# The weight ring of a two-layer encoder kernel: four slots instead of five

## The chip, the cores and the metric

The kernel runs on one core of one Trainium2 chip. The metric is the device time of one execution in microseconds (us). Three runs of the kernel before took 1249.94, 1251.59 and 1251.48 us (median 1251.48). All times below are read from one profiled execution of it.

## The reference

Two layers of a hybrid encoder on 256 tokens of 1024 channels, all in float32. Cut to what matters:

```python
for l in range(2):
    x = LN(alpha * x + 0.5 * swiglu(x, w_gate[l, 0], w_up[l, 0], w_down[l, 0]))      # D_FF = 2816
    p = x @ w_in[l]               # 2824 columns: diff-attention q, k, v; mLSTM q, k, v, gates; S5 input
    x = LN(alpha * x + concat(diff_attention(p), mlstm(p), s5(p)) @ w_out[l])
    q, kv = x @ xattn_wq[l], mem @ xattn_wkv[l]                                       # 256 memory rows
    x = LN(alpha * x + softmax(q k / 16) v @ xattn_wo[l])
    x = LN(alpha * x + 0.5 * swiglu(x, w_gate[l, 1], w_up[l, 1], w_down[l, 1]))
```

The weights, about 200 MB, are read from HBM once; activations stay in SBUF.

## The kernel before

**Units.** Each product with a weight matrix is cut into units. A unit is a piece of weights of 128 partitions by 2048 float32 columns, 1 MB (ten units are half as large). There are 198 units in one fixed order, written out by hand (`unit_order`). In the text F0 is the first FFN of a layer and F1 the second; each has 33 units, three for every block of 256 hidden channels: gate and up for the first half of the input channels, gate and up for the second half, and down. Between the FFNs stand the units of the mix (`w_in` pieces DV, DQ, DK, SU, MQ, MK, MM, then `w_out` pieces W), of the cross attention (WQ, WO), and sixteen K and V units of the memory, which need no activations and are put where TensorE (PE) would have to wait for a chain on other engines (`FILL`).

**The way of a unit.** Four engines work on it. SyncE (SP) loads it with two DMAs into a ring slot `RAW[u % RING]` (`load`, line 402). ScalarE (ACT) copies the slot to `WH[u % RING]`, rounding to the fp32r type that PE multiplies in (`split`, line 1226). VectorE (DVE) writes the rest, RAW minus WH, back over RAW as `WL` (`split`, line 1654). PE then multiplies three times per chunk (high by high, high by low, low by high: lines 518 to 520) and adds one to `unit_used` with the last matmul of the unit. The slot is free then, and not before: `load(u)` waits until `unit_used` is at least `u - RING + 1`, which with a ring of five is the end of unit u-5.

**The order on the engines.** No engine chooses its order at run time. ACT and DVE have one list each, in which the splits stand between all their other work: the SiLU and product of the FFN (`silu`, `h_mul`), the transposing of the FFN's hidden block (`turn_h` on PE in F0, sixteen DVE transposes in F1) and its own split into HH (ACT, `h_hi`) and HL (DVE, line 1650), which PE needs before the down unit; layer norms (`boundary`); RoPE (`swap_copy`, a matmul at line 908, `rope`), the S5 recurrence (`s5_states`), softmaxes (`diff_exp`, `diff_mix`), and in F0 the preparing of the S5 tables on DVE (`prepare_...`, `tables`, after blocks 0 to 6, `skip_taps` before the last). An ACT list entry "split" waits for the landing of its unit, and what stands behind it in the list waits too.

In one FFN block j the ACT list is: HH of block j, split, two SiLUs of block j+1, split, split. The DVE list is: HL of block j, split, two products of block j+1, split, (F1: the sixteen transposes of block j+1), split, (F0: a piece of table work). PE's own list is: gate/up unit, gate/up unit, wait for HH and HL, down unit.

**POOL.** GpSimd loads parameters and layer norm vectors. At the start its DMAs wait for chosen ring slots to be filled a given number of times, so that they go behind the first weights; the units meant are 2, 5, 7 and 9.

Of the kernel before, what the change touches and what calls it, by code (L numbers as in the profile page):

```python
# [44 lines left out]
LAMBDA_INIT = [0.8 - 0.6 * math.exp(-0.3 * l) for l in range(DEPTH)]  # L45


RING = 5
FFN_UNITS = 3 * BLOCKS
FILL = {("mix", 0): [(0, "K", 0), (0, "K", 1)],  # L50
# [60 lines left out]
def build(nc, x_in, mem_in, wg, wu, wd, ln_g, ln_b, w_in, w_out, wq, wkv, wo, par, const, out):  # L111
# [12 lines left out]
    with ctx:  # L124
        top = [(nc.sbuf_base + 31) // 32 * 32]

        def place(name, shape, dt, at=None):
            size = 4 * int(np.prod(shape[1:]))
            if at is None:
                at = top[0]  # L130
                top[0] += (size + 31) // 32 * 32
            return nc.alloc_sbuf_tensor_at(name, shape, dt, offset=at), at

        def sb(name, shape, dt=F32, at=None):
            return place(name, shape, dt, at)[0]
# [6 lines left out]
        ML = sb("ML", [P, KC, SEQ], F32R)  # L142
        slots = [place(f"RAW{s}", [P, 2048], F32) for s in range(RING)]
        RAW = [slot for slot, _ in slots]
        WL = [sb(f"WL{s}", [P, 2048], F32R, at) for s, (_, at) in enumerate(slots)]
        WH = [sb(f"WH{s}", [P, 2048], F32R) for s in range(RING)]
        LNGB, gb_at = place("LNGB", [P, 2, D], F32)
# [104 lines left out]

        raw_loaded = [Event(f"raw_loaded{s}", 0) for s in range(RING)]
        split_hi = Event("split_hi", 0)
# [143 lines left out]
        def _(sp):  # L398
# [3 lines left out]
            def load(u, first, second):  # L402

                if u >= RING:
                    sp.wait_ge(unit_used.sem, u - RING + 1)
                for dst, src in (first, second):
                    sp.dma_start(dst, src).then_inc(raw_loaded[u % RING].sem, 16)  # L407

# [1939 lines left out]
        def _(pool):  # L2348
# [86 lines left out]
            def load_params(l):  # L2435

                pool.dma_start(PAR[:, :], par[l, :, 0:P_END]).then_inc(param_in.sem, 16)
                pool.dma_start(PDL[:, :], par[l, :, P_DL:P_DL + 256]).then_inc(param_in.sem, 16)
                if l == 0:
                    pool.wait_ge(raw_loaded[0].sem, 64)  # L2440
                pool.dma_start(PB[96:128, :, :, :].rearrange("c (a i) t n -> c a (i t n)", a=4),
                               par[l, :, P_B:P_B + 512].rearrange("(a c) n -> c a n", a=4)).then_inc(rest_in.sem, 16)
                pool.dma_start(PCB[:, :], par[l, :, P_C:P_C + 1024]).then_inc(rest_in.sem, 16)
                pool.dma_start(iota[:, :], const[:, K_IOTA:K_IOTA + STEPS]).then_inc(rest_in.sem, 16)

            pool.wait_ge(raw_loaded[2].sem, 32)
            load_params(0)
            pool.wait_ge(raw_loaded[2].sem, 64)
            pool.dma_start(kst[:, P:K_END], const[:, P:K_END]).then_inc(const_rest.sem, 16)
            pool.wait_ge(raw_loaded[4].sem, 64)  # L2450
            for l in range(DEPTH):
                count["n"] = 0
                layer["l"] = l
# [22 lines left out]
                if l + 1 < DEPTH:  # L2476
                    load_params(l + 1)
# [72 lines left out]
```

## Time and profile before

| | |
|---|---|
| time, median of three runs | 1251.48 us |
| the profiled execution: its own time | 1249.85 us |
| its span | 1248.0 us |
| PE busy | 1226.9 us (98%) |
| DVE busy | 874.5 us (70%) |
| ACT busy | 600.0 us (48%) |
| POOL busy | 156.1 us (13%) |
| read from HBM | 217.34 MB, 175 GB/s over the span |
| chain that ended last | PE 96%, all else 4% |

The span is what the profile covers, the time holds 1.85 us more around it. Busy time counts instructions of an engine; the granted TensorE clock was 0.999 over the span. The chain that ended last is followed back from the last instruction, at each step to what released it.

### The profile page before, as it was taken

How to read it: one execution, taken by the hardware profiler on the slowest of the kernel's cores; microseconds unless marked ns; L12 is line 12 of the kernel's file. 1: busy time of each engine (PE TensorE's matmuls, PEld its weight loads, DVE VectorE, ACT ScalarE, POOL GpSimd, SP SyncE). 2: the span in 40 equal slices, each digit the busy share in tenths (PEclk: the TensorE clock that was granted, in tenths of full speed). 3: DMA queues.
4: the chain of work that ended last, by engine and by line, in shares of the span. 5: the costliest groups of instructions: out<-in, count | busy, mean ns of one | idle time of the engine just before them, and what ended most of it. 6: DMA issues, size and time to landing. Idle time of an engine off the chain costs nothing.

```text
span 1248.0 us, 16328 instructions
## 1 busy us (share of the span) xinstructions
PE 1226.9 (98%) x6616; PEld 1052.0 (84%) x6616; DVE 874.5 (70%) x1337; ACT 600.0 (48%) x731; POOL 156.1 (13%) x161
## 2 busy tenths in 40 slices
PE   7999999999999999999999999999999999999997
PEld 6888888998889888888888888889987998788886
DVE  5677747687565668888856676665776756988885
ACT  5444554557444554443445344545556445544442
POOL 1026800000102000000000067300001100000000
PEclk9999999999999999999999999999999999999999
DMA  9755555542456366566666555645323635655560
GB/s 336 266 169 188 183 169 169 169 131 72 138 200 216 102 228 210 186 187 200 202 203 193 179 197 174 192 151 185 113 102 120 196 124 158 212 187 186 200 203 34
DMA packets 160234, 219.45 MB, mean 176 GB/s; under 512 B 6912, under 2 KB 136064, under 8 KB 160160
## 3 DMA queue, kind: packets, MB, share of 16 engines
q1 hardware_dynamic: 156864, 206.60, 51.0%
q0 software_dynamic: 3152, 11.76, 2.9%
q8 instruction: 52, 0.85, 0.3%
q14 instruction: 22, 0.18, 0.0%
q10 hardware_dynamic: 144, 0.07, 0.0%
HBM read 217.34 MB, written 1.05 MB: 175 GB/s over the span
## 4 chain that ended last, share of the span: by engine, by line
PE 96%; SPq 1%; DMA 1%; issue 1%; ACT 1%; DVE 1%; DVEq 0%; POOLq 0%; POOL 0%
PE PS L518 28%; PE PS L520 28%; PE PS L519 28%; PE PS L1141 1%; PE PS L1165 1%; PE PS L601 1%; PE PS L931 1%; PE PS L549 1%; DMA RAW<-in_ffn_w_down 1%; SPq L407 1%; PE PS L831 1%; PE PS L843 1%; PE PS L864 1%; PE PS L908 1%; PE PS L781 0%
## 5 line engine op out<-in xcount | busy, mean ns | idle before, releaser
L1650 DVE TENSOR_TENSOR WL<-RAW,WH 128x2048 fp32r<-128x2048 f32 (+1 forms) x199 | 447.4, 2254 | 170.4 <-ACT WH L1222 169.3
L1222 ACT ACTIVATE WH<-RAW 128x2048 fp32r<-128x2048 f32 (+1 forms) x199 | 370.8, 1872 | 164.4 <-DMA RAW<-in_ffn_w_up 129.3
L518 PE MATMUL PS<-WH,XH 128*128 128x512 f32 x762 | 302.3, 397 | 1.7 <-DVE WL L1650 1.4
L520 PE MATMUL PS<-WH,XL 128*128 128x512 f32 x762 | 297.3, 390 | 0.0
L519 PE MATMUL PS<-WL,XH 128*128 128x512 f32 x762 | 297.2, 390 | 0.0
L518 PEld LDWEIGHTS PS<-WH,XH 128*128 128x128 f32 x762 | 143.4, 188 | 32.5 <-DVE WL L1650 1.8
L520 PEld LDWEIGHTS PS<-WH,XL 128*128 128x128 f32 x762 | 143.2, 188 | 30.3
L519 PEld LDWEIGHTS PS<-WL,XH 128*128 128x128 f32 x762 | 143.5, 188 | 28.8 <-issue 0.5
L518 PE MATMUL PS<-WH,HH 128*128 128x512 f32 x352 | 137.8, 392 | 1.2 <-issue 1.1
L520 PE MATMUL PS<-WH,HL 128*128 128x512 f32 x352 | 137.1, 389 | 0.0
L519 PE MATMUL PS<-WL,HH 128*128 128x512 f32 x352 | 137.0, 389 | 0.0
L1810 DVE STREAM_TRANSPOSE PS<-HB 32x128 f32<-32x128 f32 x320 | 103.3, 323 | 4.7
L518 PE MATMUL PS<-XH,WH 128*128 128x256 f32 x320 | 94.1, 294 | 0.0
L2420 POOL TENSOR_TENSOR SM<-SM,half_c 128x1 f32<-128x1 f32 x16 | 12.9, 804 | 643.8 <-DVE SM L1705 643.8
L519 PE MATMUL PS<-XL,WH 128*128 128x256 f32 x320 | 90.5, 283 | 0.0
L520 PE MATMUL PS<-XH,WL 128*128 128x256 f32 x320 | 90.5, 283 | 0.0
L1316 ACT ACTIVATE SG<-PS 128x256 f32<-128x256 f32 x88 | 33.7, 383 | 114.8 <-PE PS L520 114.8
L1222 ACT ACTIVATE HH<-PS 128x512 fp32r<-128x512 f32 x44 | 26.3, 599 | 112.5 <-PE PS L549 57.7
L518 PEld LDWEIGHTS PS<-WH,HH 128*128 128x128 f32 x352 | 66.1, 188 | 16.1 <-issue 2.7
L520 PEld LDWEIGHTS PS<-WH,HL 128*128 128x128 f32 x352 | 66.1, 188 | 13.9
L519 PEld LDWEIGHTS PS<-WL,HH 128*128 128x128 f32 x352 | 66.1, 188 | 13.5
L519 PEld LDWEIGHTS PS<-XL,WH 128*128 128x128 f32 x320 | 61.3, 192 | 1.6 <-issue 1.4
(352 smaller groups left out, 1790.6 us busy)
## 6 DMA issues: line engine op xcount, KB each, us to landing
RAW<-in_ffn_w_down SPq DMA_DIRECT2D x88, 512.0 KB, 4.4
RAW<-in_ffn_w_gate SPq DMA_DIRECT2D x87, 512.0 KB, 4.0
RAW<-in_ffn_w_up SPq DMA_DIRECT2D x87, 512.0 KB, 5.0
RAW<-in_w_in SPq DMA_DIRECT2D x44, 512.0 KB, 4.5
RAW<-in_xattn_wkv SPq DMA_DIRECT2D x32, 512.0 KB, 4.2
RAW<-in_xattn_wq SPq DMA_DIRECT2D x16, 512.0 KB, 4.3
RAW<-in_w_out SPq DMA_DIRECT2D x12, 512.0 KB, 4.5
RAW<-in_xattn_wo SPq DMA_DIRECT2D x12, 512.0 KB, 4.0
```

The lines of the kernel that those rows point to most:

```text
L407: sp.dma_start(dst, src).then_inc(raw_loaded[u % RING].sem, 16)
L518: nc.tensor.matmul(out_ap, sh, mh, start=first, stop=False)
L519: nc.tensor.matmul(out_ap, sh, ml, start=False, stop=False)
L520: return nc.tensor.matmul(out_ap, sl, mh, start=False, stop=last)
L549: mm = nc.tensor.transpose(PS[:, 6, fc * SEQ + t * P:fc * SEQ + t * P + P], HB[:, t, fc * P:fc * P + P], ident)
L601: mm = nc.tensor.transpose(PS[:, 4 + 2 * t + half, i * P:i * P + P], X[:, t, c * P:c * P + P], ident)
L831: mm = nc.tensor.matmul(PS[0:32, 7, j * P:j * P + P], PCB[:, o:o + 32], CQ[:, part, i, 0:TAPS, :].rearrange("p a c -> p (a c)"), start=(pa ...
L1222: return nc.scalar.activation(dst, src, ACT.Copy)
L1316: nc.scalar.activation(SG[:, t, :], PS[:, 4 + t, 0:FB], ACT.Silu).then_inc(sg_done.sem, 1)
L1650: return v.tensor_tensor(dst, full, hi.bitcast(F32), ALU.subtract)
L1810: ins = v.transpose(dst[:, :, :, 32 * i:32 * i + 32], src[:, :, :, 32 * j:32 * j + 32])
L2420: g.tensor_tensor(SM[:, 22 + t:23 + t], SM[:, 20 + t:21 + t], half_c[:, 0:1], ALU.pow).then_inc(ln_root.sem, 1)
```

## The change

The ring gets four slots for RAW/WL and four for WH. Everything that is placed behind them in SBUF moves down by one slot of each. `load(u)` waits for the end of unit u-4. The order of units and every engine's list stay as they are. POOL's three waits name another slot and count: slot 1 filled twice is unit 5 (before slot 0 twice), slot 3 twice is unit 7 (before slot 2 twice), slot 1 three times is unit 9 (before slot 4 twice).

```diff
-RING = 5
+RING = 4
...
                 if l == 0:
-                    pool.wait_ge(raw_loaded[0].sem, 64)
+                    pool.wait_ge(raw_loaded[1].sem, 64)
...
             load_params(0)
-            pool.wait_ge(raw_loaded[2].sem, 64)
+            pool.wait_ge(raw_loaded[3].sem, 64)
             pool.dma_start(kst[:, P:K_END], const[:, P:K_END]).then_inc(const_rest.sem, 16)
-            pool.wait_ge(raw_loaded[4].sem, 64)
+            pool.wait_ge(raw_loaded[1].sem, 96)
```

## Rows read from the trace of the kernel before

**Rows 1.** Page, busy us (share of the span) and instructions of each engine.

```profile
PE 1226.9 (98%) x6616; PEld 1052.0 (84%) x6616; DVE 874.5 (70%) x1337; ACT 600.0 (48%) x731; POOL 156.1 (13%) x161
```

**Rows 2.** Waits of SP's queue: waited for: us in total, times, longest us.

```profile
SPq L407 <- PE PS L520: 1000.5, 190, 21.6
```

**Rows 3.** Page, costliest groups: busy, mean ns of one | idle before, releaser.

```profile
L1650 DVE TENSOR_TENSOR WL<-RAW,WH 128x2048 fp32r<-128x2048 f32 (+1 forms) x199 | 447.4, 2254 | 170.4 <-ACT WH L1222 169.3
L1222 ACT ACTIVATE WH<-RAW 128x2048 fp32r<-128x2048 f32 (+1 forms) x199 | 370.8, 1872 | 164.4 <-DMA RAW<-in_ffn_w_up 129.3
```

**Rows 4.** Page, DMA issues: count, KB each, median us to landing.

```profile
RAW<-in_ffn_w_down SPq DMA_DIRECT2D x88, 512.0 KB, 4.4
...
RAW<-in_ffn_w_up SPq DMA_DIRECT2D x87, 512.0 KB, 5.0
```

**Rows 5.** Timeline of SP's queue, F1 of layer 0: start us, us, issue.

```profile
510.86 0.38 SPq L407 DMA_DIRECT2D RAW<-in_ffn_w_gate  x1
...
527.18 0.38 SPq L407 DMA_DIRECT2D RAW<-in_ffn_w_gate  x1
```

**Rows 6.** Timeline of DVE, the same block: start us, us, operation.

```profile
515.41 5.37 DVE L1810 STREAM_TRANSPOSE PS<-HB 32x128 f32<-32x128 f32 x16
```

**Rows 7.** Timelines of SP's queue and DVE, a block of F0, layer 1.

```profile
727.88 0.37 SPq L407 DMA_DIRECT2D RAW<-in_ffn_w_gate  x1
...
739.24 0.38 SPq L407 DMA_DIRECT2D RAW<-in_ffn_w_gate  x1
...
729.64 2.47 DVE L1650 TENSOR_TENSOR WL<-RAW,WH 128x2048 fp32r<-128x2048 f32 x1 [2.68 <-ACT WH L1222]
...
735.99 0.69 DVE L1650 TENSOR_TENSOR HL<-PS,HH 128x512 fp32r<-128x512 f32 x1
```

**Rows 8.** Timelines of SP's queue and DVE, start of F1, layer 0.

```profile
464.03 0.38 SPq L407 DMA_DIRECT2D RAW<-in_ffn_w_gate  x1
...
469.05 0.42 DVE L1799 TENSOR_TENSOR HB<-SG,PS 128x256 f32<-128x256 f32 x1
```

**Rows 9.** Timelines of SP's queue, ACT and PE, around the SU unit, layer 0.

```profile
242.02 0.92 SPq L407 DMA_DIRECT2D RAW<-in_w_in  x2
...
242.41 0.58 ACT L1222 ACTIVATE XE<-PS 128x512 f32<-128x512 f32 x1
...
244.70 1.02 PE L908 MATMUL PS<-XE,kst 128*128 128x512 f32 x2
```

**Rows 10.** Timelines of SP's queue, DVE and PE, from MQ on, layer 0.

```profile
260.73 0.88 SPq L407 DMA_DIRECT2D RAW<-in_w_in  x2
...
254.67 4.49 DVE L1650 TENSOR_TENSOR WL<-RAW,WH 128x2048 fp32r<-128x2048 f32 x2 [3.06 <-ACT WH L1222]
...
271.53 0.75 DVE L2051 SCALAR_TENSOR_TENSOR PR<-PR,SM 128x128 f32<-128x128 f32 x2
...
276.72 0.49 PE L942 MATMUL PS<-kst,PR 128*128 128x128 f32 x3
```

**Rows 11.** Timelines of SP's queue, ACT and PE, end of cross attention, layer 1.

```profile
1050.90 0.37 SPq L407 DMA_DIRECT2D RAW<-in_ffn_w_gate  x1
...
1045.40 1.92 ACT L1222 ACTIVATE WH<-RAW 128x2048 fp32r<-128x2048 f32 x1 [2.55 <-DMA RAW<-in_ffn_w_up]
...
1053.44 1.03 PE L601 MATMUL PS<-kst,X 128*128 128x128 f32 x8
```

**Rows 12.** Timeline of PE at the start.

```profile
11.69 0.59 PE L518 MATMUL PS<-WH,XH 128*128 128x512 f32 x1
12.12 0.39 PE L519 MATMUL PS<-WL,XH 128*128 128x512 f32 x1
12.35 0.40 PE L520 MATMUL PS<-WH,XL 128*128 128x512 f32 x1
```

**Rows 13.** Stretches: us, busy (instructions) PE PEld DVE ACT POOL, PEclk, DMA.

```profile
1240.40:1244.30 3.90, 0.00 (x0) 0.00 (x0) 3.17 (x7) 1.24 (x2) 0.55 (x1) 1.00 0.33 134
1244.30:1248.00 3.70, 0.00 (x0) 0.00 (x0) 1.27 (x2) 0.00 (x0) 0.00 (x0) 0.50 0.38 142
```

## The prediction

> **What bounds the kernel now.** I read the page's engine rows first: PE is busy 98% of the span and all others have room [rows 1]. The kernel can therefore be slower only by making PE wait. Then the waits of SP's queue: 190 loads stood, 1000.5 us in all, until PE had let go of a slot [rows 2]. So every load is issued at the end of a unit, and the ring's size sets of which one. The costliest groups come third: one split costs ACT 1.87 us and DVE 2.25 us, and ACT's idle time ahead of its splits is mostly a wait for a landing, 129.3 us [rows 3]. ACT is thus not late by its own work in the FFNs; it stands at a split until the unit is there, with its list behind it. In the timelines last I looked, at each split, for when its slot was let go and what stands behind it.
>
> **What the change moves.** 194 loads are issued one unit later. From the release to the landing a gate/up unit takes 0.42 us (its second DMA is issued that much later) and 5.0 us, 5.4 in all; a down unit 0.4 and 4.4, so 4.8 to 4.9 [rows 4]; for the `w_in`, K and V units I read 4.9 to 5.3 and for half units 3.4. A full unit of PE's work is 5.44 us, a third of the block of 16.32 between the two issues of [rows 5]. Where ACT now waits for a landing its split starts 5.4 us later. Weights themselves stay early enough: DVE finished its split 9 to 13 us before PE took the unit in the steady blocks, and 5.4 off that leaves 4 or more. What counts is what stands behind the splits in two lists that can't be reordered. I went through both lists with the release of unit u-4 in place of u-5, all durations kept, and noted where PE comes first. POOL's waits still mean the same units; its next result that PE needs had over 20 us to spare, cost 0. The lower SBUF addresses: no row connects time with an address, 0; bounds -1 and +1 us (the spread of the three runs). The terms:
>
> A. *Start of an FFN* (4 times). The first split in the FFN's list is the unit b+4 (b its first unit); behind it stand the second SiLU, the second product and, in F1, the transposes. Unit b+4 can now be issued only when unit b ends. Layer 0, F1: issue 464.03, landed 469.4, ACT to 471.4, DVE to 473.7, product at 474.1, where it ended at 469.47 before and PE used it at once [rows 8]: 4.7 us. The same sum gives 4.7 for F0 of layer 1, 3.7 for F1 of layer 1 (it already waited there 1.4 us) and 3.9 at the very start, where the queue is empty when unit 4 goes out. Together 17.0.
>
> B. *Blocks of F0 with table work on DVE.* The chain: release, landing 5.45, ACT 1.92, DVE 2.29, table work W, HL 0.68, and 0.1 for the handovers, 10.45 + W. PE has, from the release to the down unit, 739.24 - 727.88 = 11.36 us. The table work is the DVE time between the third split's end and HL: 735.99 - (729.64 + 2.47) = 3.9 in the block shown [rows 7], with which the chain is 14.1 (the landing there 5.2): PE waits 2.7. For the seven such blocks of layer 1 the waits are 3.3, 2.7, 3.4, 2.7, 2.1, 1.4, 2.4 (W from 4.3 down to 2.5; the later blocks give PE 11.8), in layer 0 3.4, 2.8, 3.6, 2.5, 2.1, 1.3, 2.4, and 0.5 in each eighth block by ACT's own table work. Each wait stands alone: the next chain starts from PE's end of the down unit. Together 37.1. The blocks without table work, and the chain to the two products (10.5 against 10.9), cost nothing while a landing takes under 5.8.
>
> C. *Last block of an FFN.* PE goes there from one down unit to the next, so the last split, 5.0 + 1.9 + 2.3 after a release, then `skip_taps` (2.1 us, F0 only) and HL end 4.2 us after PE in three of four FFNs (4.0 in layer 1's F0; the last FFN has no unit left to split): 12.3.
>
> D. *Steady blocks of F1.* DVE's chain: release, down unit landed 4.9, ACT 1.9, DVE 2.3, transposes 5.37 [rows 6], split 2.2, HL 0.68, handovers 0.2: 17.55 against PE's 16.32 [rows 5]. The chain starts at a release ahead of the wait, so a block that waited 1.2 gives the next 1.2 more: every second block pays. Nine blocks, 6.0 us for each F1, 12.0.
>
> E. *Mix.* Here the loads that ACT's list wants early are the costly ones. The split of DQ's second half stands in front of the copy XE for the swap matmul in SU: released at 242.02, it lands at 247.2, ACT is done at 249.1 and XE at 249.7, while PE comes at 244.7 [rows 9]: 4.95. The split of MM's first unit stands in front of `s5_states` on DVE: before, DVE had it in the pair at 254.67, ahead of MQ's end at 260.73; now it waits for that end, so (with PE 4.95 late) it lands at 270.8 and DVE is done at 275.1 instead of 259.1. `s5_states`, `diff_max` and `diff_mix` take the 13.2 us to 272.3 before, 288.3 now; PE wants the result at 276.7, now 282.1 [rows 10]: 6.2, and 0.45 on the way. That is 11.6 in each layer. Layer 1 has no memory units in the middle of its mix, its splits of W come long after their landing, and it pays no more. Layer 0 has four such units, and the same pattern goes on, each time a split that waits for the unit PE has just ended, with the work that PE wants next behind it: K2 and K3 before the third swap copy 0 and the fourth 4.9; V0 before the second `diff_exp` 5.0; W1 before the third 3.75; W2 before the copy AT of head 2, 6.95, and the decay scores 1.0; W3 before AT of head 3, 5.7. Together 39.1 for layer 0, 50.7 for both.
>
> F. *Around the cross attention.* WQ0's split stands before the layer norm's square: 1.4 and 1.2. The last WO unit comes 1.85 late, twice. At its end two splits stand before the square of the next norm. In layer 1 the second was done at 1045.40; now it waits for the release of 1050.90 (+1.85), so the split ends at 1060.1, square, root and scale at 1063.6, and PE, which went on at 1053.44 [rows 11], waits 8.3. Layer 0 by the same sum 5.7, where K units lie between. Together 20.3.
>
> G. *The clock.* The waits above hold 11 of 4.7 us or more. At the end of the trace PE does nothing from 1240.4 on; the granted clock is 1.00 for 3.9 us and 0.50 after that [rows 13]. So a long wait can leave PE at 1.2 GHz. Priced by the start: until 12.1 us a matmul starts every 0.43 us, after it every 0.23 [rows 12]; that went on for 4.4 us of products there, a loss of 4.4 x (1 - 0.23/0.43) = 2.0 us. Eleven times is 22; the bounds are 0 and 31 (7 us at the lower clock each). I take half, 11: not each wait need lower it, and while PE is slow the other lists catch up.
>
> The Trainium skill, "TensorE: Matmul & The Clock Gate", section "Why this matters for your kernels", says that an idle gap between bursts of matmuls puts the array back to its lower clock. By that rule G would be near its 22; the trace agrees only with its last idle stretch.
>
> Sum: A 17.0, B 37.1, C 12.3, D 12.0, E 50.7, F 20.3: 149.4; G 11: 160. On the profiled execution's 1249.85 that is 1410; the median of the runs is 1.6 us above it, so I say 1411.
>
> **Rivals.**
> 1. *The clock holds.* G is 0: 1400. For it: inside the span the granted clock never moved, with waits up to 1.4 us. Against: [rows 13].
> 2. *The clock drops at nearly each long wait and nothing is got back*: 149 + 22 to 31, so 1422 to 1431.
> 3. *The FFN lists take it up.* The waits of B, C and D are differences of a few us between two chains of 10 to 17. If landings with one slot less in flight took 3.5 instead of 5.4, D would vanish and B and C shrink by 1.9 each: 17 blocks times 1.9 less, A 8 less: about 1250 + 160 - 12 - 32 - 8, 1358. For it: the fourth and fifth load share the engines at times. Against: at one unit per 5.4 us and 5.0 to landing hardly two overlap now.
> 4. *Not slower.* Four slots are read as enough, because a unit's DVE split stays 4 us or more ahead of PE, and PE is the only bound: 1250. At the start it could even gain, with one load less ahead of the parameter loads, up to the 1.4 us that PE waits for a split there. It decides if no entry behind a waiting split is the next thing that PE needs; [rows 8] and [rows 9] show a margin of 0.1 and 1.7 us, against 5. The Trainium skill, "Trainium Kernel Development and Optimization", section "Best Practices", advises double buffering for the overlap of DMA with compute. By it four slots are plenty and the time is this rival's; the trace speaks against it with the 129 us that ACT stands at landings with five.
> 5. *More cascades than I found*: late entries met by landings of 6 us and more (they occur, up to 10.8 where POOL loads at the same time), 10 to 20% on 149: 1425 to 1450.
>
> **How the numbers follow.** Forecast 1411: 0.42. Clock holds 0.20. Clock in full 0.12. Shorter landings 0.11. More cascades 0.12. Not slower 0.02, the last 0.01 for something in between. The range 1368 to 1440 takes in rivals 1 and 2, both bounds of G, and errors of a fifth downward in the sum of A to F; outside are rival 4, the lower part of 3 and the upper part of 5. Within 0.2%, 2.5 us, is what this kernel's measurement can't tell from no change: slower 0.97, same 0.02, faster 0.01.
>
> **What would show it.** PE's busy share falls to about 88 to 90%. ACT's waits for landings grow from some 165 us to well over 300. New waits of PE: for DVE's HL in F0's blocks 1 to 7 (2 to 3.5 us each), none in F0's block 9, every second block in F1; the swap matmul at line 908 about 5 us; the transposes at line 942 in the mix; line 601 before F1 of layer 1 about 8. Layer 0's mix grows three times as much as layer 1's. The PE clock shows stretches below 1.0 behind the long waits. Wrong would be: weights themselves (DVE WL) as the main releaser of PE; the FFN blocks unchanged; landings shorter than 4.5 us.

## The result, and the profile after

| | before | four slots |
|---|---|---|
| time, median | 1250.79 us | 1462.11 us (1457.5 to 1466.46, 4 runs) |
| ratio | | 1.169, 95% interval 1.1675 to 1.1704 |
| span of the profiled execution | 1248.0 us | 1461.7 us |
| mean granted clock | 0.999 | 0.947 |

The change costs 211 us. 160 us were forecast, with a range up to 1440, and the time lies 22 us above it.

The engine rows of the profile page after, to set beside [rows 1]:

```profile
PE 1299.2 (89%) x6616; PEld 1093.9 (75%) x6616; DVE 870.2 (60%) x1337; ACT 596.0 (41%) x731; POOL 144.1 (10%) x161
```

This row splits the loss. PE does the same 6616 matmuls and is busy 72.3 us longer (1226.9 before). Its idle time is 1461.7 - 1299.2 = 162.5 us, where it was 21.1: 141.4 us more. The two make 213.7, the whole difference of the spans. Waits were forecast at 149.4 and the clock at 11, so the waits hold and the clock does not.

What PE waited for, after (us in total, times, longest us); of these only line 601 on the constants, the first wait of the kernel, was there before at this size:

```profile
PE PS L518 <- issue: 62.3, 33, 4.1
PE PS L942 <- DVE PR L2051: 20.7, 4, 5.9
PE PS L908 <- ACT XE L1222: 15.1, 4, 4.9
PE PS L518 <- DVE HB L1799: 14.3, 5, 4.2
PE PS L950 <- ACT AT L1222: 12.3, 2, 7.1
PE PS L601 <- DVE X L1711: 10.8, 2, 8.0
PE PS L518 <- DVE WL L1650: 7.6, 5, 2.2
PE PS L601 <- DMA kst<-in_constants: 4.9, 1, 4.9
```

The weights themselves (DVE WL) are 7.6 us of it. The rest are results that stand behind a split in a list: the FFN's HH and HL ahead of a down unit (most of the 33 times "issue", by which the profile means that it shows no releaser; in the block below PE starts 0.1 us behind HL), the mixed softmax PR, the swap copy XE, the product HB at an FFN's start, the copy AT, the norm's X.

Waits of SP's queue, the costliest groups and the landings, after, to set beside [rows 2 to 4]:

```profile
SPq L407 <- PE PS L520: 1222.0, 191, 22.3
```

```profile
L1650 DVE TENSOR_TENSOR WL<-RAW,WH 128x2048 fp32r<-128x2048 f32 (+1 forms) x199 | 446.5, 2247 | 437.1 <-ACT WH L1222 436.2
L1222 ACT ACTIVATE WH<-RAW 128x2048 fp32r<-128x2048 f32 (+1 forms) x199 | 371.8, 1872 | 616.2 <-DMA RAW<-in_ffn_w_up 305.1
```

```profile
RAW<-in_ffn_w_down SPq DMA_DIRECT2D x88, 512.0 KB, 4.3
...
RAW<-in_ffn_w_up SPq DMA_DIRECT2D x87, 512.0 KB, 5.0
```

ACT stands idle 616.2 us ahead of its splits, 164.4 before. A landing takes what it took: 5.0 and 4.3 us against 5.0 and 4.4.

One block of F0 in layer 1, the timelines of SP's queue, ACT, DVE and PE after (start us, us, operation, idle before and its releaser), which answers to [rows 7]:

```profile
834.36 0.38 SPq L407 DMA_DIRECT2D RAW<-in_ffn_w_gate  x1
834.78 0.51 SPq L407 DMA_DIRECT2D RAW<-in_ffn_w_up  x1
...
841.16 1.92 ACT L1222 ACTIVATE WH<-RAW 128x2048 fp32r<-128x2048 f32 x1 [11.30 <-DMA RAW<-in_ffn_w_up]
...
843.11 2.29 DVE L1650 TENSOR_TENSOR WL<-RAW,WH 128x2048 fp32r<-128x2048 f32 x1 [10.93 <-ACT WH L1222]
...
848.91 0.69 DVE L1650 TENSOR_TENSOR HL<-PS,HH 128x512 fp32r<-128x512 f32 x1
...
849.69 0.77 PE L518 MATMUL PS<-WH,HH 128*128 128x512 f32 x1 [3.99 <-issue]
```

Released and issued at 834.4, landed at 841.1 (one of the long landings, 6.8 us), ACT to 843.1, DVE to 845.4, 3.5 us of table work, HL to 849.6; PE was there at 845.7. The swap matmul in SU answers to [rows 9]:

```profile
285.98 0.92 SPq L407 DMA_DIRECT2D RAW<-in_w_in  x2
...
291.25 1.91 ACT L1222 ACTIVATE WH<-RAW 128x2048 fp32r<-128x2048 f32 x1 [5.62 <-DMA RAW<-in_w_in]
293.07 0.58 ACT L1222 ACTIVATE XE<-PS 128x512 f32<-128x512 f32 x1
...
293.70 2.08 PE L908 MATMUL PS<-XE,kst 128*128 128x512 f32 x2 [4.87 <-ACT XE L1222]
```

4.87 us were measured, 4.95 forecast. The row holds the second loss too: the two matmuls take 2.08 us, and took 1.02 before. The stretches around it (us, busy and instructions of PE PEld DVE ACT POOL, PEclk, DMA share, GB/s):

```profile
288.83:293.70 4.87, 0.00 (x1) 0.00 (x1) 1.53 (x3) 2.39 (x2) 0.00 (x0) 0.85 0.35 123
293.70:299.00 5.30, 5.30 (x19) 4.27 (x20) 4.36 (x5) 0.00 (x0) 0.00 (x0) 0.50 0.02 3
299.00:303.00 4.00, 4.00 (x36) 3.37 (x36) 1.63 (x8) 2.75 (x7) 0.00 (x0) 1.00 0.41 115
```

While PE waited the clock fell to 1.2 GHz (0.50). The counts of these rows can't be set against each other, since the shapes differ; the pace of one shape, 128x256, can. It starts every 0.21 us at 1.2 GHz and every 0.12 us at 2.4:

```profile
297.07 0.41 PE L519 MATMUL PS<-XL,WH 128*128 128x256 f32 x1
297.28 0.41 PE L520 MATMUL PS<-XH,WL 128*128 128x256 f32 x1
...
299.37 0.28 PE L519 MATMUL PS<-XL,WH 128*128 128x256 f32 x1
299.49 0.28 PE L520 MATMUL PS<-XH,WL 128*128 128x256 f32 x1
```

The trace has 26 such stretches, 150 us together, besides the one behind the last matmul. Half of 150 is 75, and PE's added busy time is 72.3.

By stages, cut at the ends of units in both traces (us; idle and busy are PE's):

| stage | before | after | more idle | more busy |
|---|---|---|---|---|
| F0, layer 0 | 205.5 | 248.5 | 27.3 | 15.7 |
| mix and cross attention, layer 0 | 249.5 | 317.0 | 43.6 | 23.9 |
| F1, layer 0 | 181.5 | 198.3 | 12.1 | 4.6 |
| F0, layer 1 | 191.3 | 235.8 | 29.1 | 15.3 |
| mix and cross attention, layer 1 | 217.1 | 248.0 | 22.0 | 8.9 |
| F1, layer 1 | 183.2 | 194.1 | 7.1 | 3.8 |

### The profile page after: what moved, and what is told of

Its sections match the earlier page's. It is cut to its first block, busy times and chain, and to the rows that moved or that the text cites. A ratio compares the mean times of both kernels' runs of the same rounds, so it can differ in the third digit from the quotient of the medians.

```text
span 1461.7 us, 16328 instructions
## 1 busy us (share of the span) xinstructions
PE 1299.2 (89%) x6616; PEld 1093.9 (75%) x6616; DVE 870.2 (60%) x1337; ACT 596.0 (41%) x731; POOL 144.1 (10%) x161
## 4 chain that ended last, share of the span: by engine, by line
PE 74%; DMA 9%; issue 6%; DVE 5%; ACT 5%; SPq 1%; POOL 0%; DVEq 0%; POOLq 0%; ACTq 0%
PE PS L518 22%; PE PS L520 21%; PE PS L519 21%; ACT WH L1222 2%; DMA RAW<-in_ffn_w_up 2%; DMA RAW<-in_xattn_wkv 2%; DMA RAW<-in_w_in 2%; DVE WL L1650 2%; DMA RAW<-in_ffn_w_down 1%; PE PS L1141 1%; DMA RAW<-in_w_out 1%; PE PS L908 1%; PE PS L1165 1%; SPq L407 1%; PE PS L601 1%
## 5 line engine op out<-in xcount | busy, mean ns | idle before, releaser
L1222 ACT ACTIVATE WH<-RAW 128x2048 fp32r<-128x2048 f32 (+1 forms) x199 | 371.8, 1872 | 616.2 <-DMA RAW<-in_ffn_w_up 305.1
L518 PE MATMUL PS<-WH,XH 128*128 128x512 f32 x762 | 306.8, 403 | 15.6 <-DVE HB L1799 14.3
L518 PE MATMUL PS<-WH,HH 128*128 128x512 f32 x352 | 150.7, 428 | 62.4 <-issue 61.0
L518 PEld LDWEIGHTS PS<-WH,XH 128*128 128x128 f32 x762 | 145.4, 191 | 48.3 <-DVE HB L1799 15.3
L519 PE MATMUL PS<-WL,HH 128*128 128x512 f32 x352 | 145.4, 413 | 0.0
L520 PE MATMUL PS<-WH,HL 128*128 128x512 f32 x352 | 145.3, 413 | 0.0
L518 PEld LDWEIGHTS PS<-WH,HH 128*128 128x128 f32 x352 | 71.4, 203 | 92.0 <-issue 76.3
L518 PE MATMUL PS<-XH,WH 128*128 128x256 f32 x320 | 98.2, 307 | 0.5 <-DVE ZT L1941 0.5
L520 PEld LDWEIGHTS PS<-WH,HL 128*128 128x128 f32 x352 | 71.1, 202 | 16.5
L519 PEld LDWEIGHTS PS<-WL,HH 128*128 128x128 f32 x352 | 71.9, 204 | 14.3
L518 PEld LDWEIGHTS PS<-XH,WH 128*128 128x128 f32 x320 | 64.7, 202 | 3.2 <-issue 2.0
L520 PEld LDWEIGHTS PS<-XH,WL 128*128 128x128 f32 x320 | 64.3, 201 | 0.0
```

Source lines behind the costliest of these rows:

```text
L518: nc.tensor.matmul(out_ap, sh, mh, start=first, stop=False)
L519: nc.tensor.matmul(out_ap, sh, ml, start=False, stop=False)
L520: return nc.tensor.matmul(out_ap, sl, mh, start=False, stop=last)
L1222: return nc.scalar.activation(dst, src, ACT.Copy)
```

## The experiments

Each kernel was timed beside the kernel before, whose medians there are 1249.8 to 1250.1 us.

**1. The issue alone.** Five slots at their old places, but each load waits for the unit it would wait for with four:

```diff
-                if u >= RING:
+                if u >= RING - 1:
+                    sp.wait_ge(unit_used.sem, u - RING + 2)
+                elif u >= RING:
                     sp.wait_ge(unit_used.sem, u - RING + 1)
```

> Five slots at the old addresses, but each load from unit 4 on waits for the unit that it would wait for with four slots. POOL's own waits are those of the kernel before. Theory (the later issue alone makes the loss, by the entries behind the waiting splits and by the clock): 1462 us, within 5. Rival (the overlap of slots or the moved SBUF addresses have a part): clearly below 1462; if they had all of it, 1251.

Measured 1461.61 us (1457.24 to 1463.72), ratio 1.168 [1.166, 1.171]. The whole loss is the later issue; slots, addresses and POOL's waits have no part that shows.

**2. The FFNs' loads alone.** As 1, with `ORDER[u][1] in ("F0", "F1")` added to the condition.

> Five slots; only the loads of FFN units (F0 and F1) wait as with four. In the changed kernel PE's waits grew by 75.6 us inside the four FFNs and its busy time, by the clock, by 39.4 us. The last wait of each F0 hangs on a unit of the mix and should stay away (two times 3.7 to 4.0 us and some 3 us of clock). Theory (the parts are separate and add): 1251 + 115 - 14 = 1352 us, between 1340 and 1362, and the mix keeps its old length. Rival (parts feed each other, a late load shifts all that follow on the queue): over 1370.

Measured 1366.08 us, ratio 1.092 [1.090, 1.094], 4 us above the stated range. Layer 0's mix and cross attention kept their 249.5 us exactly. The excess is at two places that I had not counted: the first units of an FFN are loaded in the stage ahead of it, so the norm before F0 of layer 1 was late (PE waited 3.88 us, and 2.8 us more busy time) and the one before F1 of layer 1 as well (7.94 us, and 2.1). Added to 1352 these give 1369. The parts add, but a load's wait falls where its split stands.

**3. Four loads of 198.** As 1, for unit b+4 of each FFN only (term A).

> Five slots; only four loads of 198, the unit b+4 at the start of each FFN (term A), wait as with four. Theory: PE waits 3 to 4.7 us at each of the four places and the clock takes some 2 to 3.5 us behind three or four of them: 14 to 17 + 6 to 12, so 1271 to 1280 us. Rival 1 (the price of a wait is the wait itself): 1265 to 1268. Rival 2 (later loads of the ring absorb it): 1251 to 1256.

Measured 1274.57 us (1273.89 to 1274.74), ratio 1.019 [1.018, 1.021]. PE's idle time grew by 14.9 us and its busy time by 9.1. Rivals 1 and 2 of this run are out: the late loads cost their waits and three fifths more. One of the five falls of the clock in this trace (1.6 of the 9.1 us) is not at a late load. It stands behind a wait of 1.36 us in the mix of layer 1, which the kernel before has too, with no fall behind it.

**4. Matmuls in the waits.** Four slots; matmuls without use (one operand zero, or a result that is overwritten) ahead of most awaited products, each group sized to the wait of the changed kernel, for example ahead of the down unit in F0's blocks 1 to 7:

```diff
+            def keep_busy(n, b, src, first):
+                for _ in range(n):
+                    nc.tensor.matmul(bank(b), ZERO[:, :], src[:, 0:2, :].rearrange("p c n -> p (c n)"),
+                                     start=first, stop=first)
...
                     gate_up(b + 3 + 3 * j, 1)
+                    if s == 0 and j <= 7:
+                        keep_busy((13, 10, 14, 9, 7, 4, 9)[j - 1], 0, XH, False)
                     h_turned(l, s, j)
```

> Four slots as in the changed kernel; PE gets matmuls of 128x512 with no use (zeros added to its own accumulators, or results that the next product overwrites) ahead of most waits: at each FFN start 7 to 15, ahead of the down unit in F0's blocks 1 to 7 4 to 14, in each last block 7 or 14, ahead of swap copies 0 and 2 17 or 18, ahead of two attention products 28 and 20. Each group is sized to end just before the awaited result. Lines 942 and 601 get none. Theory (the added busy time of 72 us is the lower clock, and the clock falls because PE pauses): the waits stay as long, about two thirds of the 152 us at the lower clock vanish, 45 to 55 us: 1407 to 1417 us. Rival (the clock falls for another reason, such as the load of the whole chip, or filler delays the real work): 1455 or more.

Measured 1447.41 us, a miss by 30 us. The trace tells why. In the F0s, where every larger wait was filled, no stretch at 1.2 GHz is left (12 in the changed kernel), and the stages took 236.0 and 223.4 us instead of 248.5 and 235.8. But the groups at the swap copies stood at copies 0 and 2, where PE does not wait at all. They added 12.2 us, and the waits at copies 1 and 3 stayed with their stretches. So the mechanism held and my placing was wrong, which the next kernel puts right (groups at copies 1 and 3):

> The filler kernel with two groups moved, which had stood at swap copies 0 and 2 where PE doesn't wait (12.2 us of added work, 53 matmuls of 0.23 us) and now stand at copies 1 and 3, in their waits of 4.7 us. Theory (each wait over some 2 us lowers the clock, and matmuls in the wait keep it up): 12.2 us of work less and the three stretches of 7 us at the lower clock behind these waits gone (10 us), so 1425 us, 1419 to 1431. Rival (the clock in the mix falls whatever PE does there): 1435.

Measured 1431.5 us (1428.62 to 1433.12): 15.9 less than the run before it, where 22 were expected, and half a us above the range at its median. The stretches behind these three waits are gone. Of ten left, one is behind the last matmul, eight follow waits without matmuls in them (lines 942 and 601 above all), and one a last block of F0 where 2.5 us of the wait stayed unfilled.

**5. The same in the small kernel.** Kernel 3 with 15, 15, 15 and 7 matmuls in its four waits.

> The kernel with four late loads (1274.6 us), and 15, 15, 15 and 7 matmuls of 128x512 in front of the awaited product at the four places, whose results the next product overwrites; 0.23 us each, within the waits of 4.1, 4.3, 4.0 and 2.1 us. Theory (the waits cost themselves plus a stretch at the lower clock that comes from PE's pause): the waits stay, the stretches go, 1274.6 - 8 = 1266 to 1268. Rival (the stretch comes whatever PE does there): 1274 to 1276.

Measured 1268.07 us (1266.35 to 1269.69), against 1274.57 without them: 6.5 us less, at the upper end of the range. No stretch at 1.2 GHz is left in the profiled run, the fastest, but for the one behind the last matmul (five more in kernel 3). The other three runs have a mean clock of 0.996, against 0.998 there, so it may have fallen once in them. The wait at the start of F1 in layer 0, without and with the matmuls (stretches, columns as above):

```profile
474.85:479.16 4.31, 0.00 (x1) 0.00 (x0) 2.64 (x3) 3.49 (x3) 0.00 (x0) 0.78 1.10 357
479.16:484.30 5.14, 5.14 (x12) 4.05 (x13) 4.94 (x16) 0.30 (x1) 0.00 (x0) 0.52 0.08 25
```

```profile
473.82:478.08 4.26, 3.56 (x17) 2.63 (x15) 2.65 (x3) 3.42 (x3) 0.00 (x0) 1.00 1.10 358
478.08:483.22 5.14, 5.14 (x23) 4.25 (x24) 4.94 (x16) 0.31 (x1) 0.00 (x0) 1.00 0.31 82
```

The wait is the same length. In equal time behind it PE did 12 matmuls or 23, all of 128x512. ACT and DVE did the same in both kernels. This shows what lowers the clock: PE's own pause.

**6. The order of the lists.** Four slots and the loads of the changed kernel; only the splits' places among ACT's and DVE's entries differ. In the FFNs, in ACT's and DVE's lists alike (shown for DVE, where `work()` is the table work, which stood ahead of HL):

```diff
                     h_mul(l, 22 * s + 1, 0)
-                    split()
                     h_mul(l, 22 * s + 1, 1)
                     if s == 1:
                         turn_h(l, s, 0)
                     split()
+                    split()
...
+                    if work:
+                        work()
                     split()
                     h_mul(l, j * 2 + (22 * s + 3), 0)
                     h_mul(l, j * 2 + (22 * s + 3), 1)
-                    split()
                     if not last:
                         if s == 1:
                             turn_h(l, s, j + 1)
+                        split()
                         split()
```

> Four slots and the loads of the changed kernel; only the order of ACT's and DVE's lists in the FFNs differs: the split of unit b+4 comes behind the second SiLU and product (A), the last block's last split behind the last HH and HL (C), in F1 the transposes come ahead of both splits (D), and the table work comes behind HL instead of ahead of it (B). The changed kernel lost 115 us in its four FFNs, waits and clock together. Theory (order in the lists is the cause): nearly all of it comes back, 1350 us, between 1345 and 1368, and the mix keeps its loss. Rival (with four slots the weights themselves come too late once their splits stand one place later, so the wait only changes its name): above 1400, with DVE WL as PE's releaser.

Measured 1381.45 us, ratio 1.105 [1.103, 1.107]: 80.7 us less than the changed kernel, and 13 us above the range. Inside the FFNs it went as expected: F0 costs 7.7 and 3.8 us more than before the change instead of 43.0 and 44.5, F1 3.9 and 1.2 instead of 16.7 and 10.9. What the list lost outside is new: two splits now stand behind the last HL, in front of the next norm, and PE waits 3.64, 4.02 and 3.52 us at line 601.

The mix and cross attention in the same manner, as an example ACT's list at the swap copies:

```diff
                 swap_copy(l, 0)
                 split()
-                split()
                 swap_copy(l, 1)
                 evac(l, None, 0, UT[:, :, :].rearrange("p f (s k) -> p f k s", s=TAPS),
...
                 k.then_inc(u4_low.sem, 1)
+                split()
```

> Four slots; the FFN lists as in the changed kernel; in the mix each split stands one entry later (behind the second swap copy, diff_exp 0, the fourth swap copy, diff_exp 1, the AT copies of heads 2 and 3) and around the end of cross attention one split moved behind the square (ACT) and behind the sum or the variance (DVE). The changed kernel lost 98 us between the FFNs. Theory: 85 to 98 us come back, 1364 to 1377. Rival as for the FFN lists: above 1420.

Measured 1406.68 us, 55.4 less, where 85 to 98 were expected, so 30 us above the range. Layer 1's part fell from 31.0 us to 4.0, layer 0's only from 67.5 to 32.9: there three waits of 5.6, 5.1 and 4.8 us had appeared, each time behind the next split in the list. Ahead of F1 in layer 1 a unit's own split was now late, 4.2 us. Both together:

> Both sets of moved splits together, four slots. Theory: the two gains add, 1250 to 1268 us, and the clock stays up but for a wait or two. If the late issue has a cost that order can't take away: above 1290.

Measured 1327.06 us, ratio 1.060 [1.058, 1.062], so 135 us less. This is a clear miss: 59 us above the range, and above the 1290 that the expectation had named as the sign of a cost that order can't take away. The kernel after it shows that order does take most of it away. The two gains add (80.7 + 55.4 = 136.1), but both had left something. With these splits moved once more, the first memory unit's behind the third swap copy, one of the two behind the last HL behind the squares, and four others in the same way:

```diff
                 diff_turned(l, 0)
-                mid_split(l, 0)
...
                 swap_copy(l, 2)
+                mid_split(l, 0)
                 diff_evac(l, 0)
...
                 square(l, n, 1)
+                if n in (0, 3):
+                    split()
```

> Four slots; the kernel with all moved splits (1327 us), and the splits moved once more where PE still waited in it: the second split behind each FFN's last HL goes behind the squares of the norm (waits of 3.6, 3.8 and 4.1 us at line 601), in layer 0 the first memory unit's split behind the third swap copy (5.9), W2's and W3's behind diff_exp 3 and diff_evac 3 (5.2 and 4.6), before F1 of layer 1 back ahead of the second square (4.2), in F0's block 0 the second split behind HL (2.8). Theory (each late entry has its own wait and its own stretch of the lower clock): 34 us of waits and 18 to 24 us of clock come back, so 1268 to 1282. Rival (what is late by 5.4 us comes out at another place whatever the order): above 1300.

Measured 1286.75 us, ratio 1.030 [1.028, 1.032], 5 us above the range at its median. Its profiled execution is the fastest of four (1281.22, the others 1285 to 1289). What PE still waited for in it:

```profile
PE PS L518 <- DVE WL L1666: 7.8, 6, 2.1
PE PS L518 <- issue: 5.2, 6, 1.4
PE PS L518 <- DVE HB L1819: 5.2, 7, 1.6
PE PS L601 <- DMA kst<-in_constants: 5.0, 1, 5.0
PE PS L518 <- DVE CL L1666: 2.7, 1, 2.7
```

In this execution no wait but the first is over 2.7 us, and the clock never fell while PE worked. Order takes back 175 of the 211 us at the median. The three other runs are 4.3, 6.8 and 7.5 us longer, and in them the clock did fall: their mean granted clock is 0.996, 0.993 and 0.995, against 0.999 in the profiled one. From these figures they had some 8, 15 and 10 us more at 1.2 GHz, an estimate, of which half is lost time. Behind which waits it fell is not known; the profiled execution has four of 1.8 to 2.7 us, all without a fall. The same lists with five slots:

> The same lists with five slots. If the later place of the splits costs nothing by itself: 1248 to 1256. Where it costs more, PE waits for DVE WL, the weights; then the lists of the kernel before were set for five slots and those here for four, up to 1270.

Measured 1255.18 us, ratio 1.004 [1.002, 1.005]. They are slightly worse than the old ones where there are five slots (waits of 2.0 us at W3 and 1.4 at line 601), so some 31 of the 36 us that remain belong to four slots. No kernel here beats the one before.

## Why the prediction was wrong

The waits, term by term (each is the sum of PE's pauses at these places in the trace after, less what stood there before):

| term | forecast | measured |
|---|---|---|
| A, start of an FFN | 17.0 | 12.2 |
| B, F0 with table work | 37.1 | 40.6 |
| C, last block | 12.3 | 9.9 |
| D, F1 | 12.0 | 13.1 |
| E, mix | 50.7 | 47.4 |
| F, around cross attention | 20.3 | 18.2 |
| sum | 149.4 | 141.4 |
| G, the clock | 11 | 72.3 |

**Right: the path and the places.** Line 908 4.87 and 4.74 us (4.95 forecast), the first wait at line 942 5.91 and 5.90 (6.2), line 601 before F1 of layer 1 7.96 (8.3). F0's blocks 1 to 7 of layer 1 waited 3.8, 4.0, 3.4, 3.1, 1.8, 1.7 and 3.0, against 3.3, 2.7, 3.4, 2.7, 2.1, 1.4 and 2.4. Kernel 1 shows the later issue as the cause, and kernels 6 the place in the lists. With the table work moved behind HL, beside the other moves of the first kernel of 6, none of B's blocks 1 to 7 waits over 1 us. A and C came smaller in F1: A 3.1 for 4.7, then 0.9 for 3.7, and C 2.1 for 4.2 in layer 0 (none was forecast in the last FFN, and none came).

Two sums are closer than their parts. F holds a wait of 2.9 us at line 601 before F1 of layer 0 where 5.7 were forecast. D came as forecast in layer 0, where every second block waits (1.1, 1.5, 0.9, 0.8 and 0.9 us), but in layer 1 the blocks wait some 0.5 us each and two of them 1.7 and 1.1. That D's total is within 1.1 us is in part luck.

**Wrong: step G.** The text took "11 of 4.7 us or more" as the waits that can leave PE at 1.2 GHz, priced each at 2.0 us with 2.8 as bound, and then took half. (By its own terms twelve waits are that long, two in A, eight in E and two in F, and 7 us at its pace of 1 - 0.23/0.43 are 3.3 us each, not 2.8.) Three errors, all in one direction:

- *Which waits count.* The other steps had themselves forecast some eighteen more waits of 2 to 4.2 us (twelve in B alone), and G left them out. In the trace after, 43 waits of PE were over 1 us (without the one at the start), and with 26 of them the clock fell, in the wait or at most 1.5 us behind it. Counted in the same way over seven traces (the changed kernel, kernels 1 to 3 and the first three of 6):

| wait of PE, us | waits | clock fell |
|---|---|---|
| 1.0 to 1.8 | 51 | 1 |
| 1.8 to 2.6 | 39 | 22 |
| 2.6 to 3.6 | 33 | 23 |
| 3.6 and over | 70 | 70 |

The table leaves out the kernels with added matmuls and the last two of 6. In the profiled execution of the last one with four slots, four waits of 1.8 to 2.7 us had no fall.

- *What one costs.* 72.3 / 26 = 2.8 us, which was the upper bound, not 2.0.
- *What comes back.* Half was taken off because "while PE is slow the other lists catch up". They do so to a small part at most: the sum of the waits came out 8 us short of the forecast, not 36.

26 x 2.8 is the 72.3; the rest of the sum with it gives 1250 + 149 + 72 = 1471, within 1% of the measured time. The prediction's range failed because the bounds of G (0 and 31) held the price open and the number of waits fixed.

**The rivals.** *The clock holds* (0.20) and *shorter landings* (0.11) are out by the rows above. *The clock in full* was the right one in kind, but with the same wrong count (up to 1431). *More cascades* put the excess in the waits, and there was none. *Not slower*: its premise, that a unit's split stays ahead of PE, is true (WL 7.6 us of 162), and says nothing on what stands behind the split.

By the Trainium skill, "TensorE: Matmul & The Clock Gate", section "Why this matters for your kernels", idle gaps between bursts of matmuls are to be avoided because the array then goes back to its lower clock. The trace after agrees, 26 times; I had set it against a single idle stretch at the end of the trace and discounted it.

## What to carry to other kernels

When a change makes the engine that bounds the kernel wait, count every wait that the sum forecasts, down to some 2 us, and add what the lower clock takes: here 2.8 us for each of 26 falls, half again on top of the waits. A ring's size and the order of the lists that feed from it are one decision: with lists in which a "load has landed" entry stands ahead of urgent work, the load that goes out one unit later (5.4 us here, from five slots to four) delays that work by up to as much, however early the data is for its user. Matmuls without use in a wait that can't be removed keep the clock (6.5 us of 9 back for 52 matmuls), but only where the wait is: read its place from a trace first.

## What the runs showed of the hardware

In the pair of kernels 3 and 5 the fall of the clock hung on PE alone: with ACT, DVE and DMA doing the same (357 and 358 GB/s in the wait), 15 matmuls in it decided between 0.52 and 1.00. Between 1.8 and 3.6 us the wait's length alone does not tell: 45 of 72 waits had a fall, and in the trace after the wait of 3.14 us ahead of unit 119 had none and that of 2.17 ahead of unit 16 had one. What decides there stays open. It is not the same in each run of one kernel: in the last kernel of 6 with four slots the mean granted clock was 0.999 in one run and 0.993 in another. Landings took no less with one slot less in flight (5.4 and 4.9 us from release to landing, 5.5 and 5.0 before).
